# Index layer of a two-block network: other places for the indexer's dot products, and top-k rounds laid between the query and key heads

## The reference

```
q, k, v, qi, ki, wi = split(h @ w_in)        # 16 heads of 64; 8 index heads of 64; one index key; 8 weights
q = rope(rmsnorm(q, q_gain)); k = rope(rmsnorm(k, k_gain)); qi = rope(qi); ki = rope(rmsnorm(ki))
for each block of 128 query rows:
    score = sum over 8 index heads of relu(qi . ki / 8) * wi        # causal: other entries are -inf
    sel   = the 128 highest scores of each row                      # topk = min(256, 512 // 4) = 128
    out   = softmax(q . k[sel] / 8) @ v[sel]
return out @ w_o
```

## Time and profile before

| what | value |
|---|---|
| median of 3 runs | 1993.36 us |
| the profiled execution's own time | 1994.52 us |
| its span in the trace | 1992.7 us |
| mean granted TensorE clock, share of full speed | 0.981 |
| the panels q0 to v1 with what is laid between them | some 672 to 836 us in the span |
| the attention loop behind them | some 836 to 906 us |

### The profile page before, as it was taken

One profiled execution on the slowest core, in us unless ns is written; L12 is line 12 of the kernel. 1 busy time (PEld: TensorE's weight loads), 2 busy tenths in 40 slices (PEclk: granted clock), 3 DMA queues, 4 the chain that ended last, 5 costly groups with the idle time before them and its releaser, 6 DMA issues.

```text
span 1992.7 us, 25017 instructions
## 1 busy us (share of the span) xinstructions
PE 1912.3 (96%) x9679; PEld 1545.4 (78%) x9679; DVE 761.2 (38%) x1293; ACT 749.8 (38%) x1160; POOL 840.7 (42%) x413
## 2 busy tenths in 40 slices
PE   2899999999999999999999999999998999999998
PEld 1777888888888877768888888888775868888887
DVE  7984231111003369782311110020636556503621
ACT  5534242232223243783432322243458362212212
POOL 1002444443444447644444434445345444434443
PEclk8799999999999799999999999999999999999999
DMA  5014233333332222102333332333420313233331
GB/s 126 13 25 139 88 86 101 100 90 95 100 101 70 72 77 84 64 2 64 89 101 100 90 95 96 108 107 111 127 64 2 95 43 106 85 105 90 100 106 63
DMA packets 210348, 168.29 MB, mean 84 GB/s; under 512 B 19537, under 2 KB 175641, under 8 KB 210200
## 3 DMA queue, kind: packets, MB, share of 16 engines
q1 hardware_dynamic: 207120, 162.05, 27.8%
q10 hardware_dynamic: 3144, 5.08, 0.8%
HBM read 162.63 MB, written 2.13 MB: 83 GB/s over the span
## 4 chain that ended last, share of the span: by engine, by line
PE 86%; DVE 7%; ACT 3%; issue 2%; POOL 1%; SPq 1%; DMA 1%; POOLq 0%; DVEq 0%; ACTq 0%
PE PS L2064 74%; PE PS L2330 2%; PE PS L2339 2%; PE PS L2349 2%; DVE ranked L1745 1%; DVE top L1743 1%; PE PS L1968 1%; PE PS L1969 1%; PE PS L2128 1%; DVE taken L1854 1%; POOL w_lo L623 1%; PE PS L2294 0%; PE PS L2001 0%; PE PS L1989 0%; SPq L473 0%
## 5 line engine op out<-in xcount | busy, mean ns | idle before, releaser
L623 POOL TENSOR_TENSOR w_lo<-raw,w_hi 128x2048 fp32r<-128x2048 f32 x147 | 679.2, 4620 | 975.8 <-ACT w_hi L854 845.0
L854 ACT ACTIVATE w_hi<-raw 128x2048 fp32r<-128x2048 f32 x147 | 281.7, 1917 | 626.5 <-PE PS L2064 626.5
L2064 PE MATMUL PS<-xT_hi,w_hi 128*128 128x512 f32 (+1 forms) x1152 | 441.1, 383 | 1.5 <-DVE xT_lo L1550 1.1
L2064 PE MATMUL PS<-xT_lo,w_hi 128*128 128x512 f32 (+1 forms) x1152 | 438.3, 380 | 0.0
L2064 PE MATMUL PS<-xT_hi,w_lo 128*128 128x512 f32 (+1 forms) x1152 | 438.2, 380 | 0.0
L2064 PEld LDWEIGHTS PS<-xT_hi,w_hi 128*128 128x128 f32 x1152 | 216.7, 188 | 47.3 <-issue 6.4
L2064 PEld LDWEIGHTS PS<-xT_lo,w_hi 128*128 128x128 f32 x1152 | 216.6, 188 | 41.3
L2064 PEld LDWEIGHTS PS<-xT_hi,w_lo 128*128 128x128 f32 x1152 | 216.7, 188 | 40.4
L2064 PE MATMUL PS<-w_hi,xT_hi 128*128 128x512 f32 (+2 forms) x592 | 233.5, 394 | 3.8 <-DVE head_ss L1702 3.2
L2064 PE MATMUL PS<-w_hi,hT_hi 128*128 128x512 f32 x608 | 237.0, 390 | 0.0
L2064 PE MATMUL PS<-w_hi,hT_lo 128*128 128x512 f32 x608 | 236.6, 389 | 0.0
(11 more groups left out here) (340 smaller groups left out, 2069.8 us busy)
## 6 DMA issues: line engine op xcount, KB each, us to landing
raw<-in_ffn_w_gate_up SPq DMA_DIRECT2D x88, 512.0 KB, 4.9
raw<-in_ffn_w_down SPq DMA_DIRECT2D x40, 512.0 KB, 4.3
raw<-in_w_up SPq DMA_DIRECT2D x32, 512.0 KB, 4.8
raw<-in_w_down SPq DMA_DIRECT2D x32, 512.0 KB, 4.5
raw<-in_dsa_w_in SPq DMA_DIRECT2D x28, 512.0 KB, 4.2
raw<-in_w_in SPq DMA_DIRECT2D x21, 512.0 KB, 4.2
raw<-in_s_w_glu SPq DMA_DIRECT2D x16, 512.0 KB, 4.5
raw<-in_dsa_w_o SPq DMA_DIRECT2D x8, 512.0 KB, 4.3
```

The lines of the kernel that those rows point to most:

```text
L623: pool.tensor_tensor(w_lo[:, par, :], raw[:, par, :], f32(w_hi[:, par, :]), ALU.subtract).then_inc(w_split, 1)
L854: act.activation(w_hi[:, par, :], raw[:, par, :], ACT.Copy).then_inc(w_rounded, 1)
L2064: ins = mm(o, a if weights_stay else c, c if weights_stay else a, start=first and n == 0, stop=last and n == 2)
```

## The change

Three streams are reordered; no instruction is added or removed.

- TensorE: the transposes of the index key go from place 3 to place 2 of q0. Pairs 0 and 1 of the dots come behind place 3 of q0, pairs 2 to 5 behind places 4 to 7. In q1 the pairs 6, (7, 8), (9, 10), 11 come behind places 0 to 3. The transposes of q1's heads (`turn_heads(1)`) come behind place 5 of q1, where they came behind place 6.
- ScalarE: the relus follow the dots. Four come ahead of q0's first rounding and squares. In q1 all that are left (12 to 23) come ahead of the rounding. The copies of the turned heads come ahead of the square of tb 2, where they came behind it.
- VectorE: four scores come ahead of q0's heads, and pair by pair the others follow. Block 1 has 4 rounds ahead of q1's heads, one round behind each head, and 8 after them. Block 3 has 5 rounds ahead of k0's heads, 9 between them and `last_keys`, 2 behind. `choose(3)` is now in one piece, and the four row maxima stand behind it.

```diff
--- before.py
+++ after.py
@@ -1067,23 +1067,23 @@
             head_turned(0, qiT, 0)
             act.wait_ge(ki_t, 1)
             act.activation(kiT[:, :], PS[:, 0, :], ACT.Copy).then_inc(ki_t_sb, 1)
+            for i in range(4):
+                index_relu(i)
             round_run(g + 2, 1)
             for tb in range(TB):
                 head_square("q0", tb)
-                index_relu(2 * tb)
-                index_relu(2 * tb + 1)
+                index_relu(2 * tb + 4)
+                index_relu(2 * tb + 5)
             round_run(g + 3, 1)
 
             g = head_slot("q1")
-            for i in range(NI, 3 * NI - 2):
+            for i in range(12, 3 * NI):
                 index_relu(i)
             round_run(g + 2, 1)
-            index_relu(3 * NI - 2)
-            index_relu(3 * NI - 1)
             head_square("q1", 0)
             head_square("q1", 1)
+            head_turned(1, qT, 0)
             head_square("q1", 2)
-            head_turned(1, qT, 0)
             head_square("q1", 3)
             round_run(g + 3, 1)
 
@@ -1744,7 +1744,7 @@
                     if r < ROUNDS - 1:
                         link(dve.match_replace(rk, top[:, :], sc if r == 0 else rk, 3 * NEG))
 
-            def choose(b, units=()):
+            def choose(b):
 
                 n = P * (b + 1)
                 cols = slice(BLK[b], BLK[b] + n)
@@ -1755,8 +1755,6 @@
                 link(dve.tensor_reduce(above[:, :], rk, AX.X, ALU.add, negate=True))
                 link(ts(eq[:, 0:n], sc, least, BIG, ALU.is_equal, ALU.mult))
                 link(dve.tensor_tensor_scan(sn[:, 0:n], one[:, 0:1].broadcast_to([P, n]), eq[:, 0:n], above[:, 0:1], ALU.mult, ALU.add))
-                for t in units:
-                    columns_row_max(dsa_units, DSA_UNIT, t)
                 link(stt(sn[:, 0:n], sn[:, 0:n], (TOPK - n) * BIG, eq[:, 0:n], ALU.is_le, ALU.mult))
                 tt(chosen[:, cols], rk, sn[:, 0:n], ALU.subtract).then_inc(idx_chosen, 1)
 
@@ -1804,28 +1802,35 @@
                     if during is not None:
                         during(p)
 
+            for i in range(4):
+                index_score(i)
             for tb in range(TB):
                 head("q0", tb)
-                index_score(2 * tb)
-                index_score(2 * tb + 1)
-            for i in range(NI, 3 * NI):
+                index_score(2 * tb + 4)
+                index_score(2 * tb + 5)
+            for i in range(12, 3 * NI):
                 index_score(i)
+            dve.wait_ge(idx_sum, 3 * NI)
+            choose_rounds(1, 0, 4)
             for tb in range(TB):
                 head("q1", tb)
-            dve.wait_ge(idx_sum, 3 * NI)
-            choose_rounds(1, 0, ROUNDS)
+                choose_rounds(1, 4 + tb, 5 + tb)
+            choose_rounds(1, 8, ROUNDS)
             choose(1)
             choose_rounds(2, 0, ROUNDS)
             choose(2)
+            choose_rounds(3, 0, 5)
             for tb in range(TB):
                 head("k0", tb)
-            choose_rounds(3, 0, 9)
+            choose_rounds(3, 5, 14)
             for tb in range(TB):
                 last_keys(tb)
-            choose_rounds(3, 9, ROUNDS)
+            choose_rounds(3, 14, ROUNDS)
+            choose(3)
+            dve.wait_ge(idx_chosen, 3)
             dve.wait_ge(head_t, 20)
-            choose(3, [0, 1, 2, 3])
-            dve.wait_ge(idx_chosen, 3)
+            for t in range(4):
+                columns_row_max(dsa_units, DSA_UNIT, t)
             columns_dve(dsa_units, DSA_UNIT, 3 * KT, dsa_columns, 2)
             add_panel(WO_PANEL, WO_SLOT + 2, slice(0, 512))
             norm_halves(2, lambda tb: add_row(WO_PANEL + 1, WO_SLOT + 4, slice(512, D), tb), 4 * KT, 3, FIRST_BANKS + LATE_BANKS)
@@ -2298,20 +2303,22 @@
 
                 if place == 0:
                     turn_heads(0)
-                if place == 3:
+                if place == 2:
                     pe.wait_ge(ki_done, 2)
                     pe.wait_ge(head_t_sb, 1)
                     for tb in range(TB):
                         ins = tr(PS[:, 0, P * tb:P * tb + P], ki_st[:, tb, :, :].rearrange("p a d -> p (a d)"), ident[:, :])
                     ins.then_inc(ki_t, 1)
+                if place == 3:
+                    index_dots((0, 1))
                 if place >= 4:
-                    index_dots((place - 4,))
+                    index_dots((place - 2,))
 
             def index_rest(place):
 
-                if place < 5:
-                    index_dots(((4,), (5, 6), (7, 8), (9, 10), (11,))[place])
-                if place == 6:
+                if place < 4:
+                    index_dots(((6,), (7, 8), (9, 10), (11,))[place])
+                if place == 5:
                     pe.wait_ge(idx_sum, 3 * NI)
                     turn_heads(1)
```

## The result

The changed kernel takes 1995.97 us, the median of 17 runs (1994.05 to 2000.74), beside 1992.73 us for the kernel before in 17 runs (1990.47 to 1994.39). The ratio is 1.0021 with a 95% interval of 1.0013 to 1.0028: some 4 us slower, at the edge of what the prediction called measurable. It had 1996.8 us, and +3.4.

The account below looks back on a forecast made before the run. The prediction took the start of k0's heads on VectorE, on which TensorE waits, as the bound. A 3.2 us delay plus 0.2 for the clock gave +3.4 us, forecast 1996.8 us, own range 1996.2 to 1998.4, overall 1991.6 to 1998.7.

Parts of the forecast that it names:

- What bounds the kernel: TensorE's waits, 670 to 850 us: nearly everything from 780 us on follows k0's heads starting on VectorE, before at 780.21.
- The parts at nothing: Moved dots, relus, scores and roundings cost nothing; TensorE's work up to q1's end stays the same; GpSimd's queue is not reordered.
- Steps 1 and 2: VectorE, block 1 and q1: rounds can start at 723.15; q1's last head at 735.44, 0.97 late and 7 rounds ahead.
- Steps 3 and 4: VectorE: `choose(1)` starts at 745.57, 5.92 early; its compare precedes GpSimd's subtraction, costing 0.38 instead of 3.30; lead 8.84 us.
- the rival on the other side: Small GpSimd powers also hold VectorE at `choose(1)`, so block 2 starts only 0.88 early: +6.7 us, 2000.1; chance 0.07.
- Step 5: VectorE, `choose(2)`: its fifth instruction at 770.30 waits out GpSimd's subtraction (770.28 to 774.90); next work starts at 775.83.
- Step 6: VectorE: five rounds of block 3 ahead of k0's heads cost 7.58 us; the heads start at 783.41, 3.2 us later.
- The first rival: `choose(2)`: both two-tensor instructions start before GpSimd's subtraction, k0's heads 1.26 early; 1991.8 to 1993.7, say 1992.6; chance 0.17.
- TensorE behind that: k1 opens at 785.43 after 6.4 us idle; low clock costs 2.3 us; k1 ends 3.2 to 3.6 us later.
- The sentence that the delay is not taken back: After k1, nothing up to the program's end takes the delay back: +3.2 and 0.2 for the clock, +3.4 us.

Follow-up runs that it names:

- experiment 2: Changed kernel with block 3's rounds split as before (none ahead of k0's heads, 9 between them and `last_keys`, 7 behind): 1989.35 us, ratio 0.9985.
- experiment 1: Changed kernel with the last instruction of `choose(2)` moved behind the five rounds of block 3 ahead of k0's heads: 1991.76 us, ratio 1.0001.
- experiment 3: Kernel before with only the moved dots, relus and scores, the changed ScalarE order, and row maxima behind an undivided `choose(3)`: 1992.81 us, ratio 0.9998.
- experiment 4: Kernel before with only block 3's rounds split as in the change (5 ahead of k0's heads, 9 between, 2 behind): 1999.78 us, ratio 1.0035.
- experiment 5: experiment 2 with the transposes of k1's heads one row later in panel v1 (behind place 3 instead of 2): 1984.96 us, ratio 0.9965.
- experiment 7: experiment 2 with three block 3 rounds, then the last instruction of `choose(2)`, ahead of k0's heads; 8 rounds between, 5 behind: 1988.07 us, ratio 0.9979.
- 6: experiment 5 with the last instruction of `choose(2)` behind three block 3 rounds ahead of k0's heads; 8 rounds between, 5 behind: 1986.12 us, ratio 0.9969.
- 8: The changed kernel once more, unaltered, timed against the kernel before: 1995.93 us, ratio 1.0018.

## Why the prediction was right, point by point

- **What bounds the kernel: right.** k0's heads on VectorE set the end, until they come early enough that k1 opens without a wait (experiment 2). They moved by -1.34, -4.62, 0 and +7.54 us in experiments 1 to 4, and the first P.V matmul by -1.12, -4.79, 0 and +8.55.
- **The parts at nothing: right.** The dots alone change nothing (3), TensorE has no wait on scores in q0 and q1, and GpSimd's subtraction of k0's weights starts where it did (768.42, aligned 770.27, for 770.28); only its length grew, by the 0.37 us of the meeting. The subtraction before it starts 0.69 us later than before (aligned 750.68 for 749.99), which reaches no wait of TensorE.
- **Steps 1 and 2: right.** The scores end at an aligned 723.10 (forecast 723.15), q1's last head is at 735.39 (735.44).
- **Steps 3 and 4: right.** `choose(1)` starts at 745.51 (745.57) and its compare takes 0.35 us. It did so inside a power of 128x16 (741.98 to 744.91), so that power does not hold a compare, and the rival on the other side falls. An instruction with two SBUF inputs at 746.14, inside the next power (745.73 to 748.86), took its usual 0.42 us too.
- **Step 5: right in size, off in one detail.** The fifth instruction was at 770.24 aligned, 0.06 ahead of the sum, and got in; it was the sixth that waited. The prediction had allowed for that ("even where the fifth slips in, the sixth finds it"). The fifth was expected to take 5 us; it took 0.56 and the sixth 4.84. For the loss it makes 0.2 us: k0's heads came at 783.18 instead of 783.41. Experiment 1 shows that without this wait there is no loss. There was luck in it: a sum of five terms came out within 0.06 us, where some 0.6 us more of lead would have put both instructions ahead of the subtraction.
- **Step 6: right.** Five rounds cost 7.54 us (7.58) in experiment 4. In the changed kernel the fifth instruction of `choose(2)` is 8.90 us early, the meeting takes 4.28 back, and the five rounds 7.58: 2.96 late. Neither makes the delay alone. The rounds without the meeting leave 1.3 us of lead (experiment 1), and the meeting without the rounds leaves 4.6 (experiment 2).
- **The first rival: right in the sum, wrong in the way.** Experiment 1 is its case. Its time was 1991.8 to 1993.7, which is -1.6 to +0.3 us, say -0.8, and experiment 1 shows -1.12 locally and -0.7 between medians. But it had k1 open without the low clock, and then TensorE's idle ahead of k1's transposes grow to 4.2 us, with a price there. Measured are a low clock at k1 behind 1.87 us of idle, and 2.81 us ahead of the transposes with no low clock behind them. That the two errors cancel is luck.
- **TensorE behind that: right, with a loose term for the clock.** k1 opened at 785.20 with 6.14 us of idle (785.43 and 6.4), and took 0.29 us more. The prediction took 2.3 us for the clock against 1.9 before, which is 0.4, and then put 0.2 into the sum, halfway between its 3.2 and 3.6. The sum was 3.2 + 0.2; measured locally 2.97 at the opening, 3.42 at k1's transposes, 3.40 at the first P.V matmul.
- **The sentence that the delay is not taken back: right.** The ratio says +4.2 us (2.6 to 5.6), the medians +3.2. The absolute 1996.8 stands 0.8 above the measured 1995.97 mostly since it was counted from a median of 3 runs, 1993.36, and 17 runs have 1992.73. The chance of 0.73 for "within 0.2%" was given on +3.4 against a bound of 4.0; the interval lies across it, and the measurement cannot tell the two.

The Trainium skill (page "SBUF — State Buffer", section "SBUF: two separate sides") has an exclusive lock on the ports shared by VectorE and GpSimd, held for a whole instruction. The long subtraction behaves so in the four profiles in which it meets the last instruction of `choose(2)` (4.84 to 4.86 us for 0.56). The small power does not: the compare at 743.66 took its usual 0.35 us inside it. Here the measurement decides.

What stays open: whether VectorE's choice would miss the subtraction altogether with a few tenths more of lead, as the first rival had it, was not tried by itself; experiment 1 gives that case's time, not its condition. Place 3 alone, on the kernel before, was not tried either.

## What to carry to other kernels

When one engine gets ahead of the engine that sets the time, its lead is worth only what the other's next wait on it can use: here 8.8 us were won on VectorE, and TensorE's wait was 3.2. Count each piece of work that is laid ahead of that wait at its full length: the five rounds took back 7.6 of the 8.8. When work is moved earlier, look at what the other engine does at its *new* time, since here one instruction of 0.56 us with two SBUF inputs became 4.84 us long behind a GpSimd instruction of 4.6. When a wait is removed, go on to the next on the same chain: with the rounds behind k0's heads and one more row ahead of k1's transposes the kernel takes 1984.96 us, 0.35% less than before (0.22 to 0.48%).

## What the runs showed that was not expected

- VectorE's `max` and `match_replace` are not held by a subtraction on GpSimd (0.69 and 0.68 us inside it, experiment 1; the `max` at 788.76 in the earlier trace rows stands inside one from 788.09 to 792.72 too), while a compare of one SBUF tensor is (3.26 us, experiment 3; 4.22 us, experiment 5).
- The subtraction started 0.03 us behind the start of the fifth instruction, took 4.99 us instead of 4.62, and the sixth, which started 0.04 us behind the fifth's end, was held until the subtraction was over. This reads as if the waiting engine gets its turn in the gap between two chained instructions; no run tries it by itself. In `choose(3)` it is the same: a subtraction at 817.80, inside the scan, took 5.45 us, and the instruction behind the scan was held.
- Small GpSimd instructions were longer while VectorE was in certain instructions: GpSimd's compare of 128x16 at 744.99 took 0.66 us for 0.21, and the power behind it 3.13 for 2.9, while VectorE was in a scan and a two-tensor instruction.
- Executions of one kernel differ by up to 12 us (1986.94 to 1999.13 in experiment 1, 1983.79 to 1993.54 in experiment 7). Most of it goes with the granted clock: in experiment 1 the seven runs at a mean of 0.983 or more took up to 1991.77 us, the five at 0.982 or less 1994.54 and more. Not all of it does: experiment 7 has a run of 1993.49 us and one of 1987.21, both at 0.985. Behind the first P.V matmul, where all these kernels have the same program, the profiled executions take 1152.2 to 1152.3 us with no low-clock stretch up to the program's last microseconds (2, 4, 5, 6), 1154.0 to 1154.3 with 6.8 us of them (before, changed, 1), and 1155.5 to 1155.6 with 10.2 (3, 7, 8). The profiled execution before has five (35.4 to 76.3, 656.6 to 677.1, 782.9 to 786.3, 1513.3 to 1516.8, 1605.5 to 1608.9). An effect of 3 us can be read from single executions only against an anchor close by. An idle of 2.7 to 2.9 us at k1's transposes brought the clock down in experiment 7 and not in 2; 1.87 us at k1 did in experiment 1.
